# Retention's decay tables and scaled queries made in the front stage of a hybrid retention and attention backbone

## The reference, cut to what matters

```python
lg_f = jax.nn.log_sigmoid(logit_f)          # one value per head, likewise lg_b
intra = where(diff >= 0, exp(lg * max(diff, 0)), 0)
xi = exp(lg * (pos + 1)); zeta = exp(lg * (L - 1 - pos)); decay_chunk = exp(lg * L)
def step(state, qkv):
    qc, kc, vc = qkv
    s = einsum('bhid,bhjd->bhij', qc, kc) * intra
    o = einsum('bhij,bhjv->bhiv', s, vc) + einsum('bhid,bhdv->bhiv', qc, state) * xi
    state = state * decay_chunk + einsum('bhjd,bhjv->bhdv', kc * zeta, vc)
    return state, o
```

## Time and profile before

| | |
|---|---|
| median of 3 runs | 3079.29 us (3076.08 to 3084.25) |
| profiled execution | 3077.75 us, span 3075.9 us |
| PE / PEld / DVE / ACT / POOL busy | 92% / 74% / 69% / 51% / 24% of the span |
| front | 0 to about 500 us |
| retention | 501.6 to about 632 us |
| the rest (mixers, experts, attention) | from about 633 us on |

### The profile page before, as it was taken

One profiled execution on the slowest core, in us unless ns is written; L12 is line 12 of the kernel. 1 busy time (PEld: TensorE's weight loads), 2 busy tenths in 40 slices (PEclk: granted clock), 3 DMA queues, 4 the chain that ended last, 5 costly groups with the idle time before them and its releaser, 6 DMA issues. The chain is left out here.

```text
span 3075.9 us, 47738 instructions
## 1 busy us (share of the span) xinstructions
PE 2839.5 (92%) x16908; PEld 2284.8 (74%) x16908; DVE 2124.6 (69%) x2559; ACT 1563.6 (51%) x2208; POOL 731.9 (24%) x1245
## 2 busy tenths in 40 slices
PE   7999997779499999999987989999998949999998
PEld 4766686768377777777767878888887838888887
DVE  4576753844677776776755457777765489999997
ACT  3212113532165555555544456677674237777775
POOL 1000001820011121221205765656620001111111
PEclk9999998989799999999998999999999969999999
DMA  6367724444567887887862000000012479999995
GB/s 242 130 212 246 250 98 191 145 146 154 221 229 292 292 297 291 301 299 298 303 213 81 18 10 25 17 20 16 8 67 103 144 307 383 396 392 393 397 398 186
DMA packets 129838, 631.43 MB, mean 205 GB/s; under 512 B 14913, under 2 KB 29377, under 8 KB 70946
## 3 DMA queue, kind: packets, MB, share of 16 engines
q1 hardware_dynamic: 117410, 591.86, 50.8%
q0 software_dynamic: 12288, 37.75, 4.9%
HBM read 563.40 MB, written 66.16 MB: 205 GB/s over the span
## 5 line engine op out<-in xcount | busy, mean ns | idle before, releaser
L2005 DVE TENSOR_TENSOR ex_wlo<-ring,ex_whi 128x2048 fp32r<-128x2048 f32 x384 | 877.4, 2290 | 216.3 <-ACT ex_whi L1934 211.9
L1934 ACT CAST ex_whi<-ring 128x2048 fp32r<-128x2048 f32 x384 | 727.6, 1904 | 295.3 <-PE psum L1899 208.9
L1899 PE MATMUL psum<-ex_whi,ex_xh 128*128 128x512 f32 x1024 | 404.5, 395 | 4.4 <-DVE ex_xl L2019 4.4
L1899 PE MATMUL psum<-ex_whi,ex_xl 128*128 128x512 f32 x1024 | 400.0, 391 | 0.0
L1899 PE MATMUL psum<-ex_wlo,ex_xh 128*128 128x512 f32 x1024 | 399.3, 390 | 0.0
L1899 PEld LDWEIGHTS psum<-ex_whi,ex_xh 128*128 128x128 f32 x1024 | 192.5, 188 | 49.9 <-issue 11.4
L473 PE MATMUL psum<-fr_whi,fr_hh 128*128 128x512 f32 x560 | 223.6, 401 | 3.9 <-DVE fr_hl L658 2.5
L1899 PEld LDWEIGHTS psum<-ex_whi,ex_xl 128*128 128x128 f32 x1024 | 192.7, 188 | 41.0
L1899 PEld LDWEIGHTS psum<-ex_wlo,ex_xh 128*128 128x128 f32 x1024 | 192.8, 188 | 38.8
L473 PE MATMUL psum<-fr_wlo,fr_hh 128*128 128x512 f32 x560 | 217.9, 391 | 0.7 <-DVE fr_wlo L664 0.7
L473 PE MATMUL psum<-fr_whi,fr_hl 128*128 128x512 f32 x560 | 217.9, 391 | 0.0
(11 more groups left out here) (316 smaller groups left out, 6050.8 us busy)
## 6 DMA issues: line engine op xcount, KB each, us to landing
ring<-in_moe_w SPq DMA_DIRECT2D x384, 1024.0 KB, 8.5
fr_raw<-in_mod_w SPq DMA_DIRECT2D x40, 1024.0 KB, 5.5
rec_d<-fr_work SPq DMA_DIRECT2D x72, 256.0 KB, 5.9
fr_raw<-in_ev_w_in SPq DMA_DIRECT2D x14, 1024.0 KB, 5.8
ring<-rec_d SPq DMA_DIRECT2D x10, 1024.0 KB, 15.4
h_d<-ring SPq DMA_DIRECT2D x18, 512.0 KB, 3.0
fr_arena<-in_mod_w SPq DMA_DIRECT2D x8, 1024.0 KB, 11.8
ring<-mod_d SPq DMA_DIRECT2D x15, 512.0 KB, 7.5
```

The costliest lines, as they stand in the source:

```text
L1899: last = nc.tensor.matmul(g.psum[:, 2 + i % 2, :], x[:, 4 * b + k, :], w[n][:, k, :], start=(b == 0 and k == 0 and first == 0), stop=(b == ...
L1934: nc.scalar.copy(whi[m % RING][:, :, :], slot(i)[:, 4 * b:4 * b + 4, :]).then_inc(hi_set, 1)
L2005: nc.vector.tensor_tensor(wlo[n][:, :, :], slot(i)[:, 4 * b:4 * b + 4, :], whi[n][:, :, :].bitcast(F32), ALU.subtract).then_inc(lo_set, 1)
```

## The change

The logarithms and powers (`lg`, `xi`, `zeta`, `decay`) are made in `front`: `lg` is loaded near its beginning, its logarithm is made before the first tile, and ACT makes the powers in step 20, in a part of `conv_y` that is free then. In steps 22 to 31 DVE multiplies the transposed queries by `xi` for both directions (`queries_scaled`), and SP stores both products in two new parts of `rec_d`, whose rows go from 12 KB to 16 KB. Retention keeps only `intra`, loads the table behind the first record, and reads the scaled queries by DMA (`load_qx`), for step i + 1 after `c_done` of step i. A context tile is stored once.

```diff
@@ front @@
         def record(t):
-            return [t + CT] + ([t - XT] if t >= XT else [])
+            return [t + CT]
...
                 sp.dma_start(gain_row, io["norm1_g"][0:1, :]).then_inc(gain_in, 16)
+                sp.dma_start(lg[:, :], io["ret_logit"].partition_broadcast(P)).then_inc(lg_in, 16)
                 sp.dma_start(g.ident[:, :], io["ident_d"]).then_inc(g.ident_in, 16)
...
                         store(turned_to[s % 2], R_QT if chunk(s - 2) == 2 else R_KT, s - 2, turned_out[s % 2])
+                    if s - 2 in QUERY:
+                        n = s - 2 - 2 * NT
+                        sp.wait_ge(qx_set, 2 * n + 2)
+                        for d in range(2):
+                            sp.dma_start(rows(io["rec_d"], n + CT)[:, (R_QX + d) * HALF:(R_QX + d + 1) * HALF],
+                                         qx[d]).then_inc(qx_out, 16)
+                    if s == NT + 2:
+                        sp.wait_ge(h_set, NT + 1)
+                        sp.dma_start(powers, io["ret_table"][:, 4 * P:6 * P + 2]).then_inc(powers_in, 16)
                     if s + 1 in ROPED:
                         load_cs(s + 1)
...
+                def powers_made():
+                    act.wait_ge(log_set, 1)
+                    act.wait_ge(powers_in, 16)
+                    for d in range(2):
+                        for n in range(HEADS):
+                            col = lg[:, d * HEADS + n:d * HEADS + n + 1]
+                            nc.scalar.activation(xi[d][:, n * P:(n + 1) * P], powers[:, d * P:(d + 1) * P], ACT.Exp, scale=col)
+                            nc.scalar.activation(zeta[:, d * HEADS + n:d * HEADS + n + 1],
+                                                 powers[:, 2 * P + d:2 * P + d + 1], ACT.Exp, scale=col)
+                    nc.scalar.activation(decay[:, :], lg[:, :], ACT.Exp, scale=float(P)).then_inc(xi_set, 1)
...
                         evacuate(s - 1)
+                    if s == 2 * NT:
+                        powers_made()
                     if 2 <= s <= 4 * NT + 1:
                         copy_turned(s - 2)
...
+                def queries_scaled(s):
+                    n = s - 2 * NT
+                    dve.wait_ge(turn_copied, s + 1)
+                    dve.wait_ge(xi_set, 1)
+                    if n:
+                        dve.wait_ge(qx_out, 32 * n)
+                    for d in range(2):
+                        nc.vector.tensor_tensor(qx[d], turned_to[s % 2], xi[d], ALU.mult).then_inc(qx_set, 1)
...
                         rotate(s - 1)
+                    if s - 2 in QUERY:
+                        queries_scaled(s - 2)
@@ retention @@
+                def load_qx(d, i):
+                    if i >= 2:
+                        sp.wait_ge(out_sum[d], i - 1)
+                    c = (R_QX + d) * HALF
+                    sp.dma_start(qx[d][i % 2][:, :], rows(io["rec_d"], order[d][i] + CT)[:, c:c + HALF]).then_inc(
+                        qx_in[d][i % 2], 16)
...
-                sp.dma_start(lg[:, :], io["ret_logit"].partition_broadcast(P)).then_inc(lg_in, 16)
+                load_rec(XT)
                 sp.dma_start(table[:, :], io["ret_table"]).then_inc(table_in, 16)
-                load_rec(XT)
                 load_rec(XT + 1)
+                for d in dirs:
+                    load_qx(d, 0)
...
+                for d in dirs:
+                    load_qx(d, 1)
                 for i in range(2, 2 + XT // 2):
...
                     for d in dirs:
                         if i >= 1 and i + 1 < NT:
+                            load_qx(d, i + 1)
                             load_gate(d, i + 1)
...
                     pe.wait_ge(masked[d], i + 1)
-                    pe.wait_ge(qx_set[d], i + 1)
+                    pe.wait_ge(qx_in[d][b], 16 * (i // 2 + 1))
...
-                    nc.vector.tensor_tensor(qx[d][b][:, :], rec[order[d][i]][:, R_QT * HALF:(R_QT + 1) * HALF], xi[d][:, :],
-                                            ALU.mult).then_inc(qx_set[d], 1)
...
-                pool.wait_ge(tables_made, 3)
...
-                        nc.scalar.activation(intra[d][:, c], table[:, 2 * d * P:(2 * d + 1) * P], ACT.Exp, scale=col)
-                        nc.scalar.activation(xi[d][:, c], table[:, (4 + d) * P:(5 + d) * P], ACT.Exp, scale=col)
-                        nc.scalar.activation(zeta[:, n:n + 1], table[:, 6 * P + d:6 * P + d + 1], ACT.Exp, scale=col)
-                nc.scalar.activation(decay[:, :], lg[:, :], ACT.Exp, scale=float(P)).then_inc(tables_made, 1)
+                        last = nc.scalar.activation(intra[d][:, c], table[:, 2 * d * P:(2 * d + 1) * P], ACT.Exp, scale=col)
+                last.then_inc(tables_made, 1)
```

More of the change, by code:

```diff
@@ L55 @@
 EVC = 7
-R_QT, R_KT, R_K, R_V, R_GF, R_GB = range(6)
-RECW = 6 * HALF
+R_QT, R_KT, R_K, R_V, R_GF, R_GB, R_QX = range(7)
+RECW = 8 * HALF
 AH = 8
@@ L248, in stored @@
 def stored(steps, s):
-    return 16 * sum(2 if is_ctx(n) else 1 for n in steps if n <= s and n % 2 == s % 2)
+    return 16 * len([n for n in steps if n <= s and n % 2 == s % 2])
 def front(nc, io, g, conv):
@@ L276, in front @@
         sig, u = ([yf[:, 4 * D + (2 * m + b) * 256:4 * D + (2 * m + b + 1) * 256] for b in range(2)] for m in range(2))
+        lg, lga, zeta, decay = conv.lg, conv.lga, conv.zeta, conv.decay
+        free = 2 * YW
+        powers = yf[:, free:free + 2 * P + 2]
+        xi = [yf[:, free + 2 * P + 2 + d * HALF:free + 2 * P + 2 + (d + 1) * HALF] for d in range(2)]
+        assert 2 * D <= free and free + 2 * P + 2 + 2 * HALF <= 4 * D
+        qx = [yf[:, 4 * D + d * HALF:4 * D + (d + 1) * HALF] for d in range(2)]
         taps, tapb = tile("taps", [P, 4 * TAPS]), tile("tapb", [P, 4])
@@ L411, in _ @@
                 sp.wait_ge(mod_out, 32 * 6)
+                sp.wait_ge(qx_out, 32 * NT)
             @block.gpsimd
@@ L591, in _ @@
                 nc.scalar.activation(sc[:, :, 0:2], cc[:, :].rearrange("p (k s) -> p k s", s=2), ACT.Silu).then_inc(c_silu, 1)
+                act.wait_ge(logs, 1)
+                nc.scalar.activation(lga[:, :], lga[:, :], ACT.Exp).then_inc(logs, 1)
+                act.wait_ge(logs, 4)
+                nc.scalar.activation(lga[:, :], lga[:, :], ACT.Ln).then_inc(logs, 1)
                 act.wait_ge(spread, 1)
@@ L775, in retention @@
         gate = [[carve(HALF) for b in range(2)] for d in dirs]
-        intra, xi, xh, kz = ([carve(HALF) for d in dirs] for n in range(4))
+        intra, xh, kz = ([carve(HALF) for d in dirs] for n in range(3))
         sm, qx = ([[carve(HALF) if n == 0 else tile(f"qx{d}{b}", [P, HALF]) for b in range(2)] for d in dirs]
@@ L780, in retention @@
         table = tile("table", [P, 6 * P + 2])
-        lg, lga, decay = (tile(n, [P, 2 * HEADS]) for n in ("lg", "lga", "decay"))
-        zeta = tile("zeta", [P, 2 * HEADS])
+        lg, zeta, decay = conv.lg, conv.zeta, conv.decay
         stats = [tile(f"stats{d}", [P, HEADS, 6]) for d in dirs]
@@ L2914, in __init__ @@
         self.u = st.enter_context(nc.sbuf_tensor("conv_u", [P, 4, UW], F32, side="right"))
+        self.lg, self.lga, self.zeta, self.decay = (
+            st.enter_context(nc.sbuf_tensor(n, [P, 2 * HEADS], F32, side="right")) for n in ("lg", "lga", "zeta", "decay"))
 def build(nc, io):
```

38 lines of the change are left out of this document (19 added, 19 removed).

## The result

| | before | after |
|---|---|---|
| median of 8 runs each, same chip | 3077.68 us (3071.29 to 3086.93) | 3092.24 us (3089.71 to 3097.4) |
| ratio after to before, 95% interval | | 1.0049 (1.0039 to 1.006) |
| profiled execution | 3077.75 us, span 3075.9 | 3091.3 us, span 3089.2 |

The change makes the kernel slower by 0.49%, clearly over 0.3%. The forecast was 3090.0 us; by the profiled execution it is off by 1.3 us, by the median by 2.2. Up to the mixer's first transposes the kernel had lost 17.2 us against 12.2 forecast, and 3.9 came back in stages that the change doesn't touch.

A forecast was written before the change was run, and what follows sets the result against it. The prediction took PE to bound front, and in retention DVE the light steps and POOL the heavy ones. Front +4.6 and retention +7.6 made +12.2 on 3077.75, so 3090.0 us; eight in ten 3078 to 3097.

The forecast's parts named there:

- front, start: Front's beginning: the `lg` load ahead of the modulation pieces delays each; +0.5 us (0.3 to 1.0).
- front, the two pieces, less 0.4 for one store: Front: modulation pieces issued late behind query products and stores, twice; PE loses 2.1 and 2.0 us.
- retention's start: Start of retention: logarithm chain gone, ACT needs only table and eight Exp; gain 3.6 us (2.7 to 4.7).
- step 2: Heavy retention step, bounded by POOL: only about 0.3 us come off.
- step 3: Retention: queries behind 2 MB land 9.7 to 9.9 us in, outputs at low clock take 6.4; +7.5 us.
- steps 4 to 6: Light retention steps, each held by the store-to-store loop at 9.3 to 9.4 us; -2.4 us in all.
- step 7: Heavy retention step whose `normalise` starts about 0.5 us late; +0.2 us.
- step 8: Retention: queries behind 2 MB land 7.9 us in, outputs end at 14.3 at the low clock; +5.0 us.
- step 9: Retention: queries land 4.5 us in, outputs end at 10.9 against 8.3 if the clock has fallen; +2.6 us.
- The loop of 9.3 us: Light retention steps: convolution store, query landing, outputs, transpose and ACT in series sum to 9.3 us, more than POOL's 8.7.
- PE keeps its clock: Rival: in retention's waits PE keeps its clock, or half of it; +4.5 us, no change, 3082; chance 0.24.
- the queries come in time: Rival: queries land about 3 us after issue beside the 2 MB, all retention steps gain; 3066 to 3073; chance 0.06.

The follow-up runs named there:

- both ways tried: The changed kernel with query stores issued by POOL, 3100.75 us; or with SP's wait and query stores moved behind the next step's modulation pieces, 3101.25 us.
- the transposes: The changed kernel with idle PE transposes, read by nobody, ahead of the outputs of retention steps 3, 5, 8 and 9; 3086.1 us, ratio 1.0029.

## Why the prediction was right, and where it was not

It was right on the sign and the main cause, and by the medians on the size (14.6 us against 12.2). Its single terms were off by up to 3.3 us. Term by term, from the two profiled executions:

| term | forecast | measured | how |
|---|---|---|---|
| front, start | +0.5 | -0.9 | step 24's transposes 204.38, then 203.52 |
| front, the two pieces, less 0.4 for one store | +3.7 | +3.3 | from there to retention's first ACT row: 297.23, 300.54 |
| retention's start | -3.2 | -3.2 | that row to `shifted(0, 0)`: 26.58, 23.42 |
| step 1 | -1.4 | -1.3 | 10.47, 9.17 |
| step 2 | -0.3 | 0.0 | 11.76, 11.81 |
| step 3 | +7.5 | +9.6 | 10.14, 19.69 |
| steps 4 to 6 | -2.4 | +0.9 | 30.42, 31.32 |
| step 7 | +0.2 | +0.1 | 11.74, 11.81 |
| step 8 | +5.0 | +5.4 | 10.67, 16.10 |
| step 9 | +2.6 | +3.3 | 9.53, 12.81 |
| later stages | 0 | -3.9 | +17.2 at the mixer's first transposes, +13.3 in the span |

(The prediction booked the 0.4 in retention's start, -3.6.)

**Front.** The step was right in its place and its size. Measured from step 24's transposes, the piece was issued 2.2 us later than before (205.94 against 203.52, 204.64 against 204.38), as forecast. It landed after 6.1 us instead of 5.1; the sum had 0.7 for the 512 KB ahead of it, a figure that no row showed. PE waited 2.45 us at 212.08, forecast +2.1; and 1.45 and 1.05 at 248.92 and 257.08 where before it had waited 0.60 in all, forecast +2.0. The kernel with the new front alone is 3.2 us slower by its median, with 1 still at the edge of its interval, which fits but is no proof by itself. That moving the stores would save it, which the prediction didn't claim but the experiments tried, is wrong in both ways tried.

**Retention's start.** Timelines of ACT and DVE after:

```profile
510.05 2.44 ACT L1136 ACTIVATE ring<-re_table,lg 128x128 f32<-128x128 f32 x8 [4.71 <-DMA re_table<-in_ret_table]
...
512.53 2.14 DVE L999 TENSOR_TENSOR ring<-ring,re_table 128x512 f32<-128x512 f32 x2 [7.26 <-ACT ring L1136]
514.70 1.29 DVE L1008 TENSOR_TENSOR ring<-psum,ring 128x512 f32<-128x512 f32 x2
```

As forecast, the chain is table, eight Exp in 2.44 us, mask. The table was 1.7 us later than the 508.3 assumed and the two mask products took 2.14 and not 1.3, but front itself ended 2.5 us later, so the gain relative to the stage's start is 14.11 (501.60 to 515.71) less 10.64 (504.06 to 514.70), 3.5 us.

**Step 2.** The prediction put nothing on the landing of this step's own queries. They were issued at 536.63, landed 5.0 us later, and PE waited 3.07 us for them. In a heavy step POOL's chain hides most of that, so 0.3 us were lost here, but the same step took 12.5 to 13.6 us in four other kernels with the same loads ahead of it.

**Steps 3, 8 and 9.** The mechanism is shown: the queries behind 2 MB of weight. Swapping them removes step 3's and step 8's loss. In step 3 the term's one wrong part was the time of issue. The prediction had the first query issued 1.1 us before step 2's end, as the gates before; it was issued 1.6 us behind it (550.06 against 548.46), because step 2's own queries, waited for 3.07 us at 541.76, held its outputs and so the convolution's store. (In the kernel without loads the weight is issued 1.5 us before that step's end, here 1.2 behind it.) With the landing of 10.4 us outputs started 12.05 into the step instead of 9.9, which is the whole miss of 2.1; the outputs then ran for 6.4 us and the step for 1.3 more, as forecast. That the clock makes 2.6 of these 6.4 us is worked out from rows (3.8 in step 4); the transposes couldn't test it. Step 8 came out near its +5.0 by luck: outputs began 9.6 us into the step and not 7.9, since the query landed after 10.1 us and not 8.8 and was issued 0.7 ahead of the step's end and not 1.1, but they then took only 5.3 us and not 6.4. In step 9 the query landed after 4.3 us and not 3.3, 1.0 us more, while the outputs ran 0.3 us less than the 6.4 of the forecast: its miss of 0.7. The clock's part, by the transposes, is 1.2 in step 8 and 2.3 in step 9 (forecast 2.8 and 2.0).

The page "DMA: Bandwidth & Descriptors" of the Trainium skill says, under "Queues, rings and completion order", that each transfer engine takes descriptors in ring order. The traces agree: in the six kernels with this order each query issued right behind the 2 MB lands 0.6 us or more after them, 7.8 to 12.1 us after its issue. The figure of that page of the Trainium skill which the prediction weighed, 2.0 us and the bytes at 436 GB/s, an estimate, would have made the sum some 6 us lower; in this stage the trace has 10.7 us where it gives 7.4.

**Steps 4 to 6.** This is the term that failed most, by 3.3 us. The loop of 9.3 us was right for step 4 (9.30). Step 6 took 9.74, with a landing 0.4 us later. In step 5 the landing was 4.6 us instead of the 3.1 taken from the gates, PE stood 2.45 us, and its clock fell. Windows of PE alone after, in step 5:

```profile
580.00:582.00 2.00, 0.64 (x6) 1.00 0.95 227
582.00:584.00 2.00, 0.91 (x4) 0.74 0.70 268
584.00:586.00 2.00, 2.00 (x12) 0.50 0.06 22
```

The 3.1 us was read from a place where two loads are issued. Now there are four, with the second query third among them. But step 4 has the same four in the same order, and its first query landed after 3.0 us. In the six kernels with this order the first query of step 5 took 3.8 to 4.4 us and that of step 4 2.9 to 3.9; why step 5's is the slower isn't shown.

**Later stages.** Nothing was forecast and 3.9 us came back. From the mixer's first transposes to the end the kernel before took 2442.1 us and the kernel after 2438.1. All thirteen kernels have the same later stages, and in their traces this part took 2437.7 to 2442.6 us, whatever they do in front and retention. So the 3.9 us are scatter: the one trace of before is near the long end and that of after near the short one. Most of it is in the attention stage, 724.4 us before (1613.71 to 2338.13 in PE's first transposes of the stages) and 721.8 after (1630.05 to 2351.82), 721.5 to 724.9 in all. By the medians of 8 runs, which average over that, the kernel is 14.6 us slower, 2.4 over the forecast of 12.2.

**Rivals.** That PE keeps its clock gives 3086.1 when it is kept busy in four steps, still slower than before; steps 2 and 3 ran at the low clock in part even so (0.74 and 0.91 granted), so this is no full test of the rival. That the queries come in time needed a landing under 4 us in steps 3 and 8; it was 10.7 and 10.6. Where it is brought about by order alone, the time is 3074.6, and 3070.8 with the weight cut up, against the 3066 to 3073 that this rival had.

## What to carry to other kernels

A value that is made elsewhere and loaded back must be there when it is needed: price the place in the queue at which its load is issued, with all that stands ahead of it, before pricing the work it saves. Here the saved work was worth 9 us (3079.15 with the new front alone, 3070.1 without the loads) and the loads as placed cost 22 (3092.24 against 3070.1), of which a better place in the queue gave back 17.6. A wait removed by swapping two transfers comes back one step later if the large one is still ahead of the next small one; ask for the small one a step ahead, and cut the large one into pieces. A store whose buffer is reused at once waits behind a large load just as well, and issuing it from another engine didn't help here. And a difference of 3 to 4 us between single traces can be scatter: look first whether a stage that nobody changed moves as much.

## What the hardware showed that was not expected

- Two loads of 256 KB with one other of 256 KB between them, all behind 2 MB, landed 8.6 and 12.1 us after their issues in one kernel and 10.4 and 11.0 in another, the same instructions in the same order, so that the gap between the landings was 4.4 us or 1.6.
- Stores issued by POOL are held up like those of SP by the large loads that SP issued just ahead of them: in the kernel with early queries and POOL's stores they land 8.5 and 9.6 us after issue at 208, and DVE waits 5.6 and 7.3 us in place of the 1.9 and 3.7 with SP's stores. The same page of the Trainium skill, "DMA: Bandwidth & Descriptors", states, under "Issuing engines are not separate DMA queues", that DMAs of all issuing engines run on the same 16 transfer engines; these rows agree.
- How long PE waits doesn't by itself tell whether its clock falls. The wait of 2.45 us in step 5 was followed by the lower clock (0.74 in the window behind it, then 0.50), where before the change PE had rested about 1.6 us in each light step at 1.00. But in the kernel with the stores behind the pieces a wait of 2.42 us in step 5 left it at 1.00, with outputs of 0.39 us, and in the kernel with the logarithm in step 12 a wait of 1.87 us in step 7 was followed by 0.50. PE in these two:

```profile
592.08 0.46 PE L968 MATMUL psum<-ring 128*128 128x128 f32 x2 [2.42 <-issue]
593.72 0.39 PE L969 MATMUL psum<-re_state,re_qx 128*128 128x128 f32 x2
...
602.19 0.46 PE L970 MATMUL psum<-ring 128*128 128x128 f32 x2 [1.87 <-issue]
604.99 0.63 PE L971 MATMUL psum<-re_state,re_qx 128*128 128x128 f32 x2
```
